# Sums of weight quarters on VectorE in a hybrid decoder step: one instruction of 1024 columns for two of 512

## The reference, cut to what matters

```
h   = rmsnorm(x);  proj = h @ w_in                       # q, k, v, B, C, u, gate_a, gate_b
a   = sliding-window attention with sinks (q, k, v);  b = B * dwconv3(C * u)
m   = sigmoid(gate_a) * (a @ w_attn_branch) + sigmoid(gate_b) * (b @ w_conv_branch)
x  += rmsnorm(m @ w_o)
up, g = split(rmsnorm(x) @ w_ffn_up);  f = (gelu(dwconv3(up) + bias) * g) @ w_ffn_down;  x += rmsnorm(f)
x  += sigmoid(x @ w_ple_gate) * (p @ w_ple)
```

## Time and profile before

| what | value |
| --- | --- |
| device time, median of 3 runs | 2704.88 us (2704.84 to 2705.2) |
| profiled execution, span from first to last instruction | 2702.8 us |
| TensorE busy | 2682.1 us, 99% |
| VectorE busy | 2162.3 us, 80%, 3845 instructions |
| ScalarE busy | 1361.4 us, 50% |
| HBM traffic | 169 GB/s over the span |
| granted TensorE clock | 1.000 in the mean: its upper level, 2.4 GHz |

### The profile page before, as it was taken

One profiled execution on the slowest core, in us unless ns is written; L12 is line 12 of the kernel. 1 busy time (PEld: TensorE's weight loads), 2 busy tenths in 40 slices (PEclk: granted clock), 3 DMA queues, 4 the chain that ended last, 5 costly groups with the idle time before them and its releaser, 6 DMA issues.

```text
span 2702.8 us, 55262 instructions
## 1 busy us (share of the span) xinstructions
PE 2682.1 (99%) x21029; PEld 2613.8 (97%) x21029; DVE 2162.3 (80%) x3845; ACT 1361.4 (50%) x2459; POOL 144.5 (5%) x214
## 2 busy tenths in 40 slices
PE   9999999999999999999999999999999999999999
PEld 8999999999999999979999999999999999999899
DVE  5988888777753587898888888888888768789887
ACT  5444555555542255645555555555555453445354
POOL 0000000000000000000000000000000000000000
PEclk9999999999999999999999999999999999999999
DMA  6333333333354445566566655666568575565674
GB/s 225 119 118 119 111 114 115 123 130 130 120 181 141 168 140 149 189 214 177 157 189 192 188 156 168 205 185 187 154 187 294 164 242 165 163 205 167 227 263 144
DMA packets 150356, 458.29 MB, mean 170 GB/s; under 512 B 15881, under 2 KB 46481, under 8 KB 146816
## 3 DMA queue, kind: packets, MB, share of 16 engines
q1 hardware_dynamic: 125184, 367.61, 38.3%
q0 software_dynamic: 24864, 88.52, 14.7%
q10 hardware_dynamic: 144, 0.15, 0.0%
HBM read 403.37 MB, written 54.11 MB: 169 GB/s over the span
## 4 chain that ended last, share of the span: by engine, by line
PE 97%; DVE 2%; issue 1%; ACT 0%; DMA 0%; SPq 0%; DVEq 0%; ACTq 0%
PE pair L1058 76%; PE pair L1142 7%; PE pair L1023 7%; PE pair L989 3%; PE pair L803 1%; PE pair L1112 1%; PE pair L871 1%; PE pair L894 1%; PE pair L885 1%; DVE v_lo L1889 0%; PE pair L819 0%; DVE lo L1987 0%; PE pair L955 0%; DMA s_raw<-in_sstream 0%; DVE nv_s L1676 0%
## 5 line engine op out<-in xcount | busy, mean ns | idle before, releaser
L1058 PE MATMUL pair<-o_hi,v_hi 128*128 128x260 f32 x5778 | 1640.1, 284 | 1.8 <-DVE f_low L2430 0.9
L1058 PE MATMUL pair<-o_hi,v_lo 128*128 128x260 f32 x5778 | 1631.9, 282 | 0.0
L1219 ACT ACTIVATE v_hi<-s_raw 128x512 fp32r<-128x512 f32 (+1 forms) x1328 | 826.1, 626 | 1006.8 <-PE pair L1058 839.7
L1058 PE MATMUL pair<-lo,v_hi 128*128 128x260 f32 x4140 | 1170.6, 283 | 0.0
L1889 DVE TENSOR_TENSOR v_lo<-s_raw,v_hi 128x512 fp32r<-128x512 f32 (+1 forms) x1264 | 860.1, 682 | 340.7 <-ACT v_hi L1219 300.8
L1058 PEld LDWEIGHTS pair<-o_hi,v_hi 128*128 128x128 f32 x5778 | 1086.9, 188 | 15.4 <-issue 13.5
L1058 PEld LDWEIGHTS pair<-o_hi,v_lo 128*128 128x128 f32 x5778 | 1089.1, 188 | 0.0
L1058 PEld LDWEIGHTS pair<-lo,v_hi 128*128 128x128 f32 x4140 | 778.4, 188 | 0.4
L1058 PE MATMUL pair<-lo_E,v_hi 128*128 128x260 f32 x834 | 236.1, 283 | 0.0
L1058 PE MATMUL pair<-lo_A,v_hi 128*128 128x260 f32 x804 | 226.7, 282 | 0.0
L1219 ACT ACTIVATE v_hi<-s_one 128x512 fp32r<-128x512 f32 (+1 forms) x212 | 131.8, 625 | 178.9 <-PE pair L1058 153.5
(11 more groups left out here) (229 smaller groups left out, 2357.4 us busy)
## 6 DMA issues: line engine op xcount, KB each, us to landing
s_raw<-in_sstream SPq DMA_DIRECT2D x468, 512.0 KB, 4.7
s_one<-in_sstream POOLq DMA_DIRECT2D x146, 512.0 KB, 5.2
raw<-f_scr SPq DMA_DIRECT2D x12, 1040.0 KB, 7.4
s_raw<-in_sstream SPq DMA_DIRECT2D x32, 384.0 KB, 4.1
g_scr<-d_h SPq DMA_DIRECT2D x16, 520.0 KB, 2.7
g_in<-g_scr SPq DMA_DIRECT2D x32, 260.0 KB, 2.6
x_scr<-y_sb SPq DMA_DIRECT2D x8, 1040.0 KB, 4.9
s_one<-in_sstream POOLq DMA_DIRECT2D x16, 384.0 KB, 4.6
```

Of the source, the lines that this page charges most:

```text
L1058: mm = pe.matmul(out, wt[:, slot, kk * P:kk * P + P], r[:, k, :], start=j in (0, 1, 3) and k == 0 and n == 0, stop=k == nk - 1 and n == 2, ...
L1219: nc.scalar.activation(v_hi[:, n % 4, 0:width], src, ACT.Copy, scale=0.5 if u == "br" else 1.0).then_inc(v_hi_rdy, 1)
```

## The change

All four sums are made as one instruction over both halves, at the step at which the second half stood (`h == 1`); the call for `h == 0` returns at once. Each raises its semaphore by 2, so all that wait for either half now wait for the whole. New waits: `s3` waits for `s1` of its unit where VectorE makes `s1`; `s2` waits for the low part of piece 1, `s4` for the low part of piece 7, where these are split.

```diff
--- before.py
+++ after.py
@@ -1889,9 +1889,13 @@
                     ins = dve.tensor_tensor(v_lo[:, n % 4, 0:width], src, high, ALU.subtract)
                 ins.then_inc(v_lo_rdy, 1)
 
-            def quarter(u, q, h):
-                n = nk_of(u) // 2 * P
-                return s_raw[r_of(u) % 2][q][:, h * n:(h + 1) * n]
+            def quarter(u, q):
+
+                return s_raw[r_of(u) % 2][q][:, 0:nk_of(u) * P]
+
+            def first_sum(u):
+
+                return s_one[:, 0:nk_of(u) * P]
 
             def loaded(u, *qs):
                 for q in qs:
@@ -1910,35 +1914,44 @@
                         dve.wait_ge(s2_done, 2 * (u - 1 - earlier(u - 1)) + last + 1)
                 if u > U_O:
                     return
-                dve.tensor_tensor(w_src(u, 1, h), quarter(u, 2, h), quarter(u, 3, h), ALU.add)\
-                   .then_inc(s1_done, 1)
+                if h == 1:
+                    dve.tensor_tensor(first_sum(u), quarter(u, 2), quarter(u, 3), ALU.add)\
+                       .then_inc(s1_done, 2)
 
             def s3(u, h):
 
-                if u >= U_END:
+                if u >= U_END or h == 0:
                     return
                 loaded(u, 0)
-                dve.tensor_tensor(quarter(u, 2, h), quarter(u, 0, h), quarter(u, 2, h), ALU.subtract)\
-                   .then_inc(s3_done, 1)
+                if u <= U_O:
+                    dve.wait_ge(s1_done, 2 * (u - earlier(u)) + 2)
+                dve.tensor_tensor(quarter(u, 2), quarter(u, 0), quarter(u, 2), ALU.subtract)\
+                   .then_inc(s3_done, 2)
 
             def s2(u, h):
 
-                if u >= U_END:
+                if u >= U_END or h == 0:
                     return
                 if in_fp32(u, 0):
-                    dve.wait_ge(v_used, h_of(u, 0, h) + 1)
-                sum_ready_1(dve, u, h)
-                dve.tensor_tensor(quarter(u, 0, h), w_src(u, 1, h), quarter(u, 0, h), ALU.subtract)\
-                   .then_inc(s2_done, 1)
+                    dve.wait_ge(v_used, h_of(u, 0, 1) + 1)
+                else:
+                    dve.wait_ge(v_lo_rdy, s_of(u, 0, 1) + 1)
+                sum_ready_1(dve, u, 1)
+                dve.tensor_tensor(quarter(u, 0), first_sum(u), quarter(u, 0), ALU.subtract)\
+                   .then_inc(s2_done, 2)
 
             def s4(u, h):
 
+                if h == 0:
+                    return
                 loaded(u, 1)
                 if in_fp32(u, 3):
-                    dve.wait_ge(v_used, h_of(u, 3, h) + 1)
-                dve.wait_ge(s2_done, 2 * (u - earlier(u)) + h + 1)
-                dve.tensor_tensor(quarter(u, 1, h), quarter(u, 1, h), quarter(u, 0, h), ALU.subtract)\
-                   .then_inc(s4_done, 1)
+                    dve.wait_ge(v_used, h_of(u, 3, 1) + 1)
+                else:
+                    dve.wait_ge(v_lo_rdy, s_of(u, 3, 1) + 1)
+                dve.wait_ge(s2_done, 2 * (u - earlier(u)) + 2)
+                dve.tensor_tensor(quarter(u, 1), quarter(u, 1), quarter(u, 0), ALU.subtract)\
+                   .then_inc(s4_done, 2)
 
             def rows_done(u, k):
```

## The result

The changed kernel takes **2711.96 us** (median of 9 runs, 2711.46 to 2713.11), the kernel before 2704.88 us on the same chip (9 runs, 2704.74 to 2705.32). The ratio is 1.0026, with a 95% interval of 1.0017 to 1.0034: slower by 7.1 us, 0.26%. The forecast was 2707.9 us with a range to 2711.0. Its sign was right; the size was not.

A forecast was written before the change was run, and what follows sets the result against it. TensorE was taken as the bound, busy 2682.1 of 2702.8 us. Four places of late sums, 0.7 + 1.4 + 0.6 + 0.3 = 3.0 us, added to 2704.9 gave 2707.9 us, with a range of 2704.4 to 2711.0.

The forecast's parts named there:

- TensorE as the bound: Whole kernel: TensorE is busy 2682.1 us of the 2702.8 us span, so it is the bound.
- the worthlessness of VectorE's time: VectorE's queue: merging saves about 22 us over the kernel, costed at nothing behind a busy TensorE.
- The length of the merged sum: Each merged sum of 1024 columns on VectorE was taken to last 1.22 us.
- the 1.45 us from its end to the end of the low part: After a merged sum, ScalarE's split and VectorE's low part were told to end 1.45 us after the sum.
- The steady `s4`: Steady units, read in unit 56: piece 10's low part comes 1.05 us later, 1.7 us remain, so hidden.
- the rule weighed in the forecast: Grouping operations can help a saturated engine; breaking them up may finish work sooner where an unsaturated engine makes others wait.
- Terms 1 to 3: TensorE waits for late low parts behind `s4`: unit 18 +0.7 us, unit 42 +1.4 us, unit 110 +0.6 us.
- Term 4: Between units 3 and 4 the PSUM sum TensorE waits for starts at 131.6, not 131.35: +0.3 us.
- The same holds for `s2` and piece 4, ... I cost these at nothing too.: Steady units: the late merged `s2` before piece 4 and the added semaphore waits are hidden, at no cost.
- Rival C: Slower by over 0.2%: the cover of piece 10 fails in roughly 100 steady units, 2718 us; chance 0.10.
- A sign that failed: Profile after the change: TensorE's busy time stays the same within 1 us.

The follow-up runs named there:

- merged_where_covered: Changed kernel with units 0 to 18, 40 to 42 and 110 kept in halves; 2704.32 us, ratio 0.9998 to the kernel before.
- conv_products_first: Changed kernel with both convolution products (L1838) moved ahead of the low part of piece 4 in the convolution units; 2708.21 us.
- s4_halves: Changed kernel with `s4` alone back in two halves; 2706.69 us.
- s2_alone: Kernel before with `s2` alone merged at the second step, the other three sums in halves; 2706.95 us.
- s2_halves: Changed kernel with `s2` alone back in two halves; 2709.09 us.
- merged_where_exposed: Kernel before with the change in units 0 to 18, 40 to 42 and 110 alone; 2712.09 us.

## Why the prediction was wrong, by its own steps

**What held.** TensorE as the bound and the worthlessness of VectorE's time: shown by 39.6 us saved for nothing. The length of the merged sum and the 1.45 us from its end to the end of the low part: in unit 56 of the changed kernel

```profile
1504.62 1.22 DVE L1953 TENSOR_TENSOR s_raw<-s_raw,s_raw 128x1024 f32<-128x1024 f32 x1
...
1506.60 0.69 DVE L1889 TENSOR_TENSOR v_lo<-s_raw,v_hi 128x512 fp32r<-128x512 f32 x1 [0.42 <-ACT v_hi L1219]
```

1506.60 + 0.69 - (1504.62 + 1.22) = 1.45. Less the 6.6 us that TensorE had lost by then (1226.49 - 1219.88), the low part's end, 1507.29, is 1500.7; the forecast was 1500.7. The steady `s4` and all units from 19 to 39, 43 to 107 are hidden, as told.

**The rule.** VectorE was the engine with idle time that can only be late, and the runs bear out the second half of the rule weighed in the forecast: the halves in the exposed units are worth 7.6 us (2711.96 for the changed kernel, 2704.32 for `merged_where_covered`), the larger instructions elsewhere nothing that can be measured. The Trainium skill (Perfetto Trace Analysis, Optimizing Scalar/DVE Operations) puts it as "breaking up instructions may allow work to be completed sooner"; this trace agrees, by those 7.6 us.

**Terms 1 to 3.** Unit 18 cost 0.80 us at pieces 10 and 11 (0.7 forecast; it began one piece earlier than told); the 0.38 that came back at piece 12 does not hang on its `s4`, since it also comes where unit 18 keeps its halves. Unit 42 cost 1.24 at piece 10 (1.4) and 0.29 at piece 7, which the forecast did not have. Unit 110 cost 0.84 (0.6). Its rows:

```profile
2594.53 1.22 DVE L1953 TENSOR_TENSOR s_raw<-s_raw,s_raw 128x1024 f32<-128x1024 f32 x1
2596.50 0.69 DVE L1889 TENSOR_TENSOR v_lo<-s_raw,v_hi 128x512 fp32r<-128x512 f32 x1 [0.76 <-ACT v_hi L1219]
```

The end of that low part, 2597.19 less the 6.42 us of shift, is 2590.77, for 2590.8 forecast.

**Term 4 was right at its place (0.26 for 0.3) and stood alone where there were four.** I had looked for rows in which TensorE already waits 1.4 us for the PSUM sum. The sum (L2167, now L2180) is just as close behind `s3` at the starts of units 3, 5 and 6, where in the kernel before no wait for it stands among the rows. Cost: 0.33 x 3 = 1.0 us.

**The step that failed** is the cost of nothing in the sentence "The same holds for `s2` and piece 4, ... I cost these at nothing too." It tested the cover of one consumer, the low part. That was right: even in unit 8 the low part had 1.2 us to spare. But VectorE and ScalarE take their work in order, and in units 8, 11, 14 and 17 the work behind the low part (L1838, then the PSUM copy L1252) had less slack than the low part itself. Price: 3.5 us. The same test was made of `s4` ("hidden, in all such units"), read in unit 56 and carried to the units of the input projection. Merged alone, `s4` costs 0.95 us at product 2 of unit 8, behind the same copy, and 0.33 at piece 10 of unit 9. With the 1.0 us at the boundaries this is 4.5 us, and 2707.9 + 4.5 = 2712.4; the measured 2712.0 is that less the small gains of the table.

Rival C came near ("ScalarE's own evacuations queue behind the late high part"): an evacuation of ScalarE was what came late. But it had the delay in ScalarE's queue and in a hundred steady units. It was in VectorE's queue, since in `conv_products_first` the high part is as late and the copy is not, and in four units with extra work. No row had been read for the units in which VectorE does more than the steady order.

**A sign that failed.** TensorE's busy time was to stay within 1 us and rose by 3.6 (2685.7 for 2682.1). 1.7 us of it are pieces 10 and 11 of unit 41, which run in part at the lower clock of the last section (2.50 and 3.14 us for 1.99 and 1.92).

## What to carry to other kernels

When an instruction in an in-order queue gets later, list everything behind it up to the next idle time of that queue, and the deadline of each, not only that of its own consumer; do it for every kind of step in which the queue carries extra work. Merging two instructions makes the first half late at the second's place and makes what follows late at the first's place, so merge where either has cover: on an engine with idle time the saved overhead is worth nothing, and the covered places can be told from the trace (here they were told from the trace of the changed kernel, not beforehand). Two delays that each fit into a queue's slack need not fit together.

## Unexpected: the granted clock after a wait

In the up-projection TensorE waits for `s4` of unit 41, and in most of these kernels its granted clock then falls to the lower of its two levels (1.2 GHz, 0.50 of full). The table by stage of the changed kernel (columns: stretch, us, busy of PE, PEld, DVE, ACT, POOL, clock, DMA):

```profile
1198.00:1200.00 2.00, 0.00 (x0) 0.00 (x0) 2.00 (x5) 2.00 (x3) 0.00 (x0) 1.00 0.00 0
1200.00:1202.00 2.00, 1.36 (x6) 1.24 (x7) 2.00 (x3) 2.00 (x4) 0.00 (x0) 1.00 0.00 0
1202.00:1204.00 2.00, 2.00 (x6) 1.55 (x6) 1.96 (x3) 0.23 (x1) 0.00 (x0) 0.50 0.00 0
1204.00:1206.00 2.00, 2.00 (x8) 1.63 (x7) 2.00 (x4) 1.71 (x3) 0.00 (x0) 0.65 0.00 0
```

The kernel before, the stretch after its own wait of 2.6 us, stays at the upper level:

```profile
1194.00:1196.00 2.00, 1.57 (x7) 1.43 (x8) 2.00 (x6) 2.00 (x4) 0.00 (x0) 1.00 0.00 0
1196.00:1198.00 2.00, 2.00 (x10) 1.53 (x9) 2.00 (x3) 1.09 (x3) 0.00 (x0) 1.00 0.00 0
```

The length of the wait alone does not decide it: `merged_where_covered` has the same wait of 2.6 us and falls to 0.50; of the kernels with a wait of 2.0 us `s4_halves` stays at the upper level and `s2_alone` falls. In the changed kernel TensorE is 2.2 us further behind after pieces 10 and 11 of unit 41 (0.5 by the longer wait, 3.1 us for 2.6, and 1.7 by slow matmuls), and the next wait, 1.9 us for L2163 in the earlier trace rows, is gone in exchange; VectorE is the limit there, so the lower clock costs next to nothing. In `s2_halves` and `merged_where_exposed` it lasts longer (0.50 from 1198 to 1204 us and from 1200 to 1206), and at most 0.6 us of it is left at the start of unit 42. What sets it off is open; no run here was made for it.
